# Reordering the halves, turns and rotations between and inside two layers, and starting the experts' gates two units later

## The reference

```
h    = rms_norm(x, g_mix[layer])
qkv  = h @ w_in[layer]                       # 1024 x 3072
o_a, o_b, o_c = differential, moba and dilated attention (rotary q and k), 4 + 4 + 8 heads
x    = x + concat(o_a, o_b, o_c) @ w_out[layer]
h2   = rms_norm(x, g_ffn[layer])
x    = x + (silu(gate) * val) @ w_down[layer],   gate, val = conv3(h2 @ w_up[layer])
```

## Time and profile before

| | us |
|---|---|
| median of three executions | 1775.79 |
| lowest, highest | 1773.83, 1776.22 |
| the profiled execution, its own time | 1779.4 |
| its span, first to last instruction | 1777.5 |
| mean granted clock of TensorE | 0.989 of full speed |
| PE busy | 1702.1 (96%) |
| DVE, ACT, POOL busy | 1146.9 (65%), 820.8 (46%), 705.2 (40%) |
| first layer, second layer, second block up to the experts, experts | about 0 to 352, 352 to 690, 690 to 986, 986 to 1777 |

### The profile page before, as it was taken

The page is one execution under the profiler, slowest core; times in us unless marked ns, Lnnn a source line. Parts: engine busy times, 40 slices in busy tenths (PEclk is TensorE's granted clock), DMA queues, the critical chain, the costliest instruction groups (busy, mean ns, idle before and its releaser), DMA issues.

```text
span 1777.5 us, 27226 instructions
## 1 busy us (share of the span) xinstructions
PE 1702.1 (96%) x10714; PEld 1461.6 (82%) x10714; DVE 1146.9 (65%) x2426; ACT 820.8 (46%) x1451; POOL 705.2 (40%) x384
## 2 busy tenths in 40 slices
PE   7999999989999999988999999899999999999997
PEld 5778998767799987543569999899999988888885
DVE  6654785746457666567332799999999644444444
ACT  5445655344466643011443554444444445445443
POOL 2324667043256740333144799700000144444442
PEclk9999999999999999999999999999999999999999
DMA  7333555553245554323345556544444566666664
GB/s 289 107 101 113 178 179 179 164 190 107 95 154 178 190 190 155 114 80 95 95 143 201 178 166 197 171 144 143 143 143 143 158 188 198 192 197 192 189 193 139
DMA packets 77455, 283.20 MB, mean 159 GB/s; under 512 B 8720, under 2 KB 8976, under 8 KB 77072
## 3 DMA queue, kind: packets, MB, share of 16 engines
q1 hardware_dynamic: 76032, 276.50, 48.2%
q10 hardware_dynamic: 1296, 4.97, 0.7%
HBM read 279.33 MB, written 2.10 MB: 158 GB/s over the span
## 4 chain that ended last, share of the span: by engine, by line
PE 70%; DVE 17%; ACT 5%; issue 4%; POOL 3%; DMA 1%; POOLq 0%; DVEq 0%; ACTq 0%
PE bank L538 55%; PE bank L529 7%; PE bank L593 5%; DVE H L1437 2%; ACT wh L1090 2%; POOL wl L2096 2%; DVE att L1448 2%; DVE H L1970 1%; DVE H L1976 1%; DVE H L1972 1%; ACT att L1093 1%; DVE wl L1431 1%; DVE H L1968 1%; DVE H L1974 1%; PE bank L661 1%
## 5 line engine op out<-in xcount | busy, mean ns | idle before, releaser
L2096 POOL TENSOR_TENSOR wl<-raw,wh 128x1024 fp32r<-128x1024 f32 x213 | 545.8, 2573 | 723.5 <-ACT wh L1090 701.8
L538 PE MATMUL bank<-hh,wh 128*128 128x256 f32 x1856 | 526.4, 284 | 3.8 <-POOL wl L2096 3.0
L1090 ACT ACTIVATE wh<-raw 128x1024 fp32r<-128x1024 f32 x476 | 492.6, 1050 | 62.0 <-PE bank L538 47.8
L538 PE MATMUL bank<-hl,wh 128*128 128x256 f32 x1856 | 519.7, 280 | 0.0
L538 PE MATMUL bank<-hh,wl 128*128 128x256 f32 x1856 | 518.7, 279 | 0.0
L1431 DVE TENSOR_TENSOR wl<-raw,wh 128x1024 fp32r<-128x1024 f32 x263 | 349.8, 1336 | 96.6 <-ACT wh L1090 96.2
L538 PEld LDWEIGHTS bank<-hh,wh 128*128 128x128 f32 x1856 | 349.8, 188 | 4.9 <-POOL wl L2096 3.9
L538 PEld LDWEIGHTS bank<-hl,wh 128*128 128x128 f32 x1856 | 349.8, 188 | 0.0
L538 PEld LDWEIGHTS bank<-hh,wl 128*128 128x128 f32 x1856 | 349.6, 188 | 0.0
L1437 DVE TENSOR_TENSOR acl<-H,ach 128x256 fp32r<-128x256 f32 x128 | 87.5, 684 | 181.6 <-ACT ach L1093 181.6
L538 PE MATMUL bank<-wh,ach 128*128 128x512 f32 x512 | 199.3, 389 | 0.4 <-DVE acl L1437 0.4
(11 more groups left out here) (217 smaller groups left out, 2326.1 us busy)
## 6 DMA issues: line engine op xcount, KB each, us to landing
raw<-in_ut_dram SPq DMA_DIRECT2D x128, 512.0 KB, 3.5
raw<-in_vt_dram SPq DMA_DIRECT2D x128, 512.0 KB, 3.6
raw<-in_wup_dram SPq DMA_DIRECT2D x88, 512.0 KB, 4.1
raw<-in_win_dram SPq DMA_DIRECT2D x48, 512.0 KB, 4.4
raw<-in_wdown_dram SPq DMA_DIRECT2D x44, 512.0 KB, 4.2
raw<-in_wout_dram SPq DMA_DIRECT2D x24, 512.0 KB, 3.6
raw<-in_wga_dram SPq DMA_DIRECT2D x16, 512.0 KB, 3.5
raw<-in_wpq_dram SPq DMA_DIRECT2D x16, 512.0 KB, 4.7
```

Of the source, the lines that this page charges most:

```text
L538: m = p.e.matmul(out, lhs[i][a], rhs[i][b], start=start and i == 0 and j == 0, stop=stop and i == n - 1 and j == 2)
L1090: a.e.activation(high_of(u), raw_of(u), ACTF.Copy).then_inc(act_hi.up(("hi", u)), 1)
L2096: g.e.tensor_tensor(low_of(u), raw_of(u), high_of(u).bitcast(F32), ALU.subtract).then_inc(pool_lo.up(("lo", u)), 1)
```

## The change

It touches only the order and the place of work; no operation is added or taken away.

1. `J_TURN` (29, 55) becomes (30, 57) and `J_GATE` 57 becomes 59. The low halves of ut units 57 and 58 go from DVE to POOL with it.
2. The causal group's turn of the attention output (`OUT_TURNS`) moves from behind w_out's unit 5 to ahead of it, on PE, ACT and DVE, in both layers.
3. In both layers ACT and DVE copy the turned q and k ahead of `stream` of the same step.
4. POOL rotates the causal group ahead of its `stream` of w_in's unit 23, in both layers.
5. Between the layers: the low halves of w_in's units 1 and 3 of layer 1 go from POOL to DVE; POOL no longer leaves out `stream` at w_down's units 19 and 20; DVE's `stream` of w_down's last unit comes behind the norm of tile 1; ACT and DVE drop `stream` of the row behind it, so that these halves come a step later; PE turns tile 1 ahead of unit 3 for tile 0 instead of behind it; DVE makes tile 1's low half ahead of its copy of the slab's first bank.

```
-        J_TURN = (29, 55)
-        J_GATE, N_GR = 57, 64
+        J_TURN = (30, 57)
+        J_GATE, N_GR = 59, 64
...
+            elif i in (first["win", 1] + 1, first["win", 1] + 3):
                 lower.append("d")
...
-        OUT_TURNS = {0: (DIFF, DIL0), 1: (DIL1, ), 6: (CAUSAL, )}
+        OUT_TURNS = {0: (DIFF, DIL0), 1: (DIL1, ), 5: (CAUSAL, )}
...                                                      # by_tokens
+                        if n in skew[:1] and (h, t) == at and between:
+                            between()
                         if t == 0:
                             unit(i)
-                        elif n in skew[:1] and h == 0 and between:
-                            between()
...                                                      # pe, w_in of layer 1
-                                  between=(lambda: turned(("n", 1), mix, 8, (1,), ...)) if L else None)
+                                  between=(lambda: turned(("n", 1), mix, 8, (1,), ...)) if L else None, at=(3, 0))
...                                                      # pe; act and dve alike
+                    if j == 5:
+                        for g in OUT_TURNS[5]:
+                            out_turned(g, (0, ))
                     out_unit(j, (0, 1), between)
-                for g in OUT_TURNS[6]:
-                    out_turned(g, (0, ))
...                                                      # act and dve, step k of w_in
+                    qk_turned(QK_TURNS.get(k, ()))
                     stream(first["win", L] + k)
...
-                    qk_turned(QK_TURNS.get(k, ()))
...                                                      # act, behind w_down
-                stream(first["row", "n", 1] if L == 0 else first["row", "g"])
+                if L:
+                    stream(first["row", "g"])
...                                                      # dve, k == 0 of layer 1
+                        turned(("n", 1), (1,), 2)
                         v.wait_ge(pe_out, ("mm", ("win", L), 0, 0))
                         copy(qkv[:, 0, 0:512], ps(("win", L), 0, 0), ("ev", "win", L, 0, 0), alone=True)
-                        turned(("n", 1), (1,), 2)
...                                                      # dve, w_down
-                    if t:
+                    if t and (L or f < NTILE - 1):
                         stream(first["wdown", L] + f)
...
                             scale(("n", 1), t, mix, first["row", "n", 1])
-                stream(first["row", "n", 1] if L == 0 else first["row", "g"])
+                            if t:
+                                stream(first["wdown", L] + f)
+                if L:
+                    stream(first["row", "g"])
...                                                      # pool, step k of w_in
-                    stream(first["win", L] + k)
+                    if k < 23:
+                        stream(first["win", L] + k)
                     if k in ROPES and ROPES[k] != DIFF:
...
+                    if k == 23:
+                        stream(first["win", L] + k)
...                                                      # pool, w_down
-                    if t and f not in (NTILE - 3, NTILE - 2):
+                    if t:
                         stream(first["wdown", L] + f)
```

More of the change, by code:

```diff
@@ L235, in program @@
             elif first["ut"] <= i < first["vt"]:
+                lower.append("d")
+            elif i in (first["win", 1] + 1, first["win", 1] + 3):
                 lower.append("d")
@@ L570, in turned_whole, with by_tokens @@
                         emptied[b] = (dve_out if q else act_out, ("hT", st, t, q))
-            def by_tokens(tag, u0, n_slabs, cw, nu, kper, off, ready, empties, of=range(8), skew=(), between=None, whole=hTw):
+            def by_tokens(tag, u0, n_slabs, cw, nu, kper, off, ready, empties, of=range(8), skew=(), between=None, at=(0, 1), whole=hTw):
                 for n in range(n_slabs):
@@ L754, in pe @@
                                   lambda n, t: (act_out if t else dve_out, ("ev", "win", L, n, t)), of=slab_banks, skew=(0,),
-                                  between=(lambda: turned(("n", 1), mix, 8, (1,), lambda t, q: (dve_out, ("nrm", ("n", 1), t, q)))) if L else None)
+                                  between=(lambda: turned(("n", 1), mix, 8, (1,), lambda t, q: (dve_out, ("nrm", ("n", 1), t, q)))) if L else None, at=(3, 0))
                 for k in range(24):
@@ L1202, in act @@
                         att_step(c)
+                    if j == 5:
+                        for g in OUT_TURNS[5]:
+                            out_turned(g)
                     stream(first["wout", L] + j)
-                for g in OUT_TURNS[6]:
-                    out_turned(g)
                 st, ev = ("f", L), ("xa", L)
```

## The result

| | before | after |
|---|---|---|
| median of four executions each, us | 1774.81 | 1756.65 |
| lowest, highest | 1773.7, 1776.22 | 1754.88, 1757.62 |
| the profiled execution, its span | 1779.4, 1777.5 | 1756.8, 1755.0 |
| mean granted clock in it | 0.989 | 0.993 |

The ratio is 0.9896, with a 95% interval of 0.9879 to 0.9913: faster by about 18.4 us (15.4 to 21.5). Forecast were 1752.6 and 1748.0 to 1761.5: the measured 1756.65 lies inside, 4.1 us above the forecast. The forecast gain, 23.2 us, lies above the interval of the measured one. The two spans differ by 22.5 us, 0.7 less than that; the medians differ by only 18.2. Where the missing 4 to 5 us went is the question of the experiments.

A forecast was written before the change was run, and what follows sets the result against it. PE was taken to bound the kernel, busy 1702.1 of 1777.5 us, losing time to stalls and low clock. Terms 7.1 + 5.6 + 3.0 + 3.3 + 4.2 = 23.2 off 1775.8 gave 1752.6 us, range 1748.0 to 1761.5.

The forecast's parts named there:

- border: Between the layers, low halves shared by DVE and POOL start tile 1 sooner: 7.1 us (5.4 to 8.0).
- experts: At the second routing, slabs 55 and 56 fill PE's 5.73 us wait: 5.6 us gained (4.0 to 7.0).
- causal turn: In both layers, w_out's unit 5 covers the turn, copy and low half: 2 x 1.50 = 3.0 us (1.5 to 3.0).
- rotation: In layer 0, POOL's rotation ahead of the low half removes PE's 1.73 us wait and low clock: 3.3 us (1.7 to 3.5).
- copies: Copying turned q and k ahead of low halves shortens PE's waits, with low clock: 4.2 us (1.5 to 4.5).
- Rival (a): At the border, DVE's unit 1 waits for POOL's unit 0: gain there 5.4, total 21.5, 1754.3 us; chance 0.15.
- Rival (d): In the gates, DVE's longer turn sets the pace, from a mean of 4.06 us; slower than before; chance 0.02.
- PE had stood still 1.73 us or longer just before: Reading of the profile before: clock falls follow such stalls, and none follows the stalls of 1.50 us or less.
- clock term: Low clock counted behind stalls: copies 1.56, rotation 1.6, border 3.0, experts 1.5, together 7.7 us of the sum.
- Rival (b): The clock's falls move to the shorter stalls that stay: 15.5 us gained, 1760.3 us; chance 0.12, with cases between.

The follow-up runs named there:

- the whole change without part 4: The changed kernel with POOL making the low half ahead of the causal group's rotation again: 1757.96 us on average.
- the transposes in the routing: The kernel before plus 45 transposes of a constant on PE in the wait of 5.73 us for the second routing: ratio 0.9984.
- parts 1, 2, 3 and 5 alone: Four runs, each the kernel before with one edit: between the layers 0.9955, experts' turns and gates 0.9970, causal turn 0.9982, q and k copies ahead of halves 0.9977.
- part 3: The kernel before with only the causal turn moved ahead of w_out's unit 5, on PE, ACT and DVE: ratio 0.9982.
- the border part alone: The kernel before with only the changes between the layers: ratio 0.9955, from five executions.
- part 2: The kernel before with only the experts' change, turns at 30 and 57 and gates from 59: ratio 0.9970.
- parts 1, 2, 4 and 5 alone: Four runs, each the kernel before with one edit: between the layers 0.9955, experts 0.9970, POOL's rotation ahead of the low half 0.9995, copies ahead of halves 0.9977.

## Why the prediction held, and where it failed

| step | forecast | measured alone | in the two profiles |
|---|---|---|---|
| border | 7.1 | 8.0 (5.2 to 10.8) | 7.3 |
| experts | 5.6 | 5.3 (3.4 to 7.5) | 5.2 |
| causal turn | 3.0 | 3.2 (1.4 to 4.8) | 2 x 1.50 |
| rotation | 3.3 | 0.9 (-1.1 to 2.8) | 3.1 (profile of the part alone) |
| copies | 4.2 | 4.1 (2.0 to 6.2) | |
| sum, or the whole | 23.2 | 21.5; whole 21.6 | 22.5 |

The last column: border as worked out above; experts from a matmul in the first routing to the first one of the second table, 1417.03 - 1066.46 = 350.57 before (the earlier trace rows has the latter) and 1394.10 - 1048.73 = 345.37 after. The lines, first of before, then two of after:

```profile
1417.03 0.47 PE L538 MATMUL bank<-wh,ach 128*128 128x512 f32 x1 [0.39 <-DVE acl L1437]
...
1048.73 0.39 PE L540 MATMUL bank<-hh,wh 128*128 128x256 f32 x1 [1.33 <-POOL wl L2105]
1394.10 0.47 PE L540 MATMUL bank<-wh,ach 128*128 128x512 f32 x1 [0.39 <-DVE acl L1442]
```

Four terms came out within 1 us, with intervals of 2 to 3 us to either side, and the parts add up to the whole. That the spans of the two profiles differ by nearly the forecast sum is in part luck: 1.5 of the 22.5 us comes between the same matmuls of the second block up to the experts (after is 698.02 - 681.76 = 16.3 us ahead at its first wait, and 1066.46 - 1048.73 = 17.7 ahead in the experts), which no edit touches.

- **Border, right.** DVE first, POOL blocked, no idle time over 1 us, clock 1.00. Rival (a) didn't come about: the low half of DVE took 1.22 us and not 2.14.
- **Experts, right in kind.** Two waits on POOL, forecast as 0.9 and 0.9, measured 0.31 and 1.29: 1.6 against the forecast 1.7 in sum (0.9 + 0.9, rounded). The first unit came sooner and the second later, as the profile's first routing had it (0.29 and 1.29). DVE's longer turns in the gates cost nothing that shows: from the first group of gates to the second table after takes 1394.10 - 1144.28 = 249.82 us, and before 1417.03 - 1161.61 (the end of the earlier trace rows's last line) = 255.42 with two more slabs of 2.81, so 249.80 without them. Rival (d) is far off.
- **Rotation, the term that was mis-sized.** The prediction gave 1.7 for the stall and 1.6 for the clock behind it, as if every execution paid the fall. The stage gained 3.1 in the profile, and the kernel 0.9 on average, 1.3 inside the whole change. The stall's part stands (1.64 in the profiles of the whole change with and without it). The clock's part was counted at its full 1.6, and most executions seem not to pay it: the same wait of 1.73 to 1.75 us is in seven profiles (before, the whole change without part 4, the transposes in the routing, and parts 1, 2, 3 and 5 alone), and the fall stands behind it in two of them (before, part 3).
- **"PE had stood still 1.73 us or longer just before", the reading under every clock term.** It held in the one profile of before, as long as PE had work (one more fall, at 1769 to 1776, comes behind its last matmul and costs nothing). It isn't a rule: in the profile of the border part alone PE stands still 1.74 us at 66.70, as in before at 66.68, and the clock stays. The window there, first of before:

```profile
66.00:74.00 8.00, 6.97 (x32) 5.43 (x32) 2.85 (x10) 2.83 (x7) 3.35 (x2) 0.79 0.28 73
```

  The same window with the border part alone:

```profile
66.00:74.00 8.00, 6.61 (x42) 5.12 (x42) 3.33 (x13) 3.12 (x7) 3.35 (x2) 1.00 0.27 71
```

  And the kernel after shows falls without a long stall, the first behind 1.09 us (at 397.11, a wait that before has too, 1.08 at 412.61, there with 1.00), the second while PE was busy all the time. Two windows of the kernel after:

```profile
396.00:406.00 10.00, 8.23 (x43) 6.32 (x42) 3.55 (x11) 3.21 (x8) 3.37 (x2) 0.83 0.23 75
736.00:746.00 10.00, 10.00 (x43) 5.34 (x43) 6.37 (x7) 0.20 (x1) 5.23 (x6) 0.66 0.24 81
```

  The program is the same in two profiles of the whole change, and even so the falls differ. The same two windows of the second one (the run of the whole change again), and the second of them in the first one, where the fall is missing:

```profile
396.00:406.00 10.00, 8.64 (x54) 6.93 (x55) 5.13 (x16) 3.82 (x10) 3.11 (x2) 1.00 0.22 61
786.00:796.00 10.00, 7.35 (x40) 3.31 (x39) 9.51 (x20) 1.68 (x3) 4.69 (x2) 0.83 0.17 52
...
786.00:796.00 10.00, 7.36 (x43) 3.56 (x44) 9.38 (x21) 1.68 (x3) 4.70 (x2) 1.00 0.17 52
```

  What the profiles show of the four clock terms is how often each is paid where its stall was left as it was: behind 1.74 us at 66.68 in 4 of 7 profiles, behind the rotation's 1.73 in 2 of 7, behind the border's 4.64 in 7 of 7 (in two of them for a shorter time), behind the routing's 5.73 in 6 of 6. So the two long stalls always had their fall and the two short ones only sometimes. With these shares the forecast's clock terms would be 1.56 x 4/7 + 1.6 x 2/7 + 3.0 + 1.5 = 5.9 instead of 7.7, and the sum 21.4, where 21.6 was measured; this is an estimate made after the fact, from few profiles.

  Rival (b), that the falls go elsewhere, would have cost 7.7 us, and the whole is 1.6 short (23.2 forecast, 21.6 measured). Falls at places where before has none do occur (412 and 698 in the profile of part 2), but that the stalls which stayed brought them about isn't shown. Split by the slope of 1.71 us for each 0.001, the five parts alone give 5.5 us of clock and 16.0 of the rest, where the forecast had 7.7 and 15.5. The whole change (mean clock 0.9893 to 0.9938) gives 7.7 and 13.9. The two splits differ by 2 us, which is within their error, so by the times alone which side the 1.6 is missing on stays open.
- **From the sum to the time, the step that made most of the 4 us.** The prediction took the sum off the median of three (1775.8), since "the stalls are in the program's order and not in that difference". True of the stalls; but 7.7 us of the sum were low clock, and what sets one execution of before apart from another is low clock too (1.71 us for each 0.001). The median of three lies 2.5 us below the mean of 67, by the slope a sample with little of it (the clocks of those three are not on record; the four executions of after that were measured with them average 1756.45, and the four of later 1756.86, so it wasn't a chip on which everything is faster). So the forecast's 4.1 us are 2.5 of a low starting point and 1.6 of a sum too large. Taken off the profiled execution the same sum gives 1756.2, where after's eight executions have 1756.66 on average; the prediction had this number and put it aside. That it comes so close is in part luck: the profiled execution lies 1.1 above the mean of 67, which makes up for most of the 1.6.

What is shown is that the low clock makes most of the spread, and that a stall of one length may or may not be followed by it. Not shown is what decides. Leaving out the fall behind PE's last matmul, the profiles of before and of part 3 alone have the same six falls; those of parts 1, 2, 4 and 5 alone lack one or more of them at stalls that the part left as they were. The Trainium skill (TensorE: Matmul & The Clock Gate, Part 1: The HAM clock gate) says that the number of matmuls at the low clock at a kernel's start varies from run to run. The number at the start wasn't looked at here; what varies here lies in mid-kernel, as the two profiles of one program show, and the mean granted clock was 0.986 to 0.992 over the 67 executions of before.

## What to carry to other kernels

Sum the idle time of a stall at its full length, but the low clock behind it only at the share of executions that pay it, and take that sum off a mean of many executions. Where there is one profile only and the clock terms are in it at full size, take the sum off the execution whose rows it was read from. Don't mix the two. Where three engines feed PE at a border between stages, give the first units to two of them (5.7 us here). Look also where the norm's short steps stand among the long halves: with three halves on POOL ahead of it the root of tile 1 came at 349.12 and DVE's `scale` waited 2.96 us for it, though moving the root by itself wasn't tried. A few transposes of a constant in a wait that can't be removed can be worth more than the wait suggests, but look in the timeline that they lie in it.

## What the runs showed of the hardware that was not expected

- One stall, several outcomes: 1.74 us idle at 66 to 67 was followed by a clock of 0.79 over 66 to 74 in before, and by 1.00 in the profile of the border part alone; over all seven profiles with this stall the fall came four times. Two profiles of the same program (the whole change) don't agree on it at 397 and at 790 either.
- A fall with PE at 10.00 of 10.00 us busy (736 to 746, clock 0.66), amid matmuls on 32 rows. It cost next to nothing: PE's wait for the table behind it was 1.42 us instead of 4.33 before, so the slow work ran in time that would have been idle. From the 32-row matmuls to the turn behind the wait it is 748.62 - 737.35 = 11.27 us after and 764.55 - 753.60 = 10.95 before. The turn, first of before, then of after:

```profile
764.55 0.44 PE L885 MATMUL bank<-ids,tab 128*128 128x128 f32 x2 [4.33 <-ACT tab L1093]
...
748.62 0.44 PE L888 MATMUL bank<-ids,tab 128*128 128x128 f32 x2 [1.42 <-ACT tab L1096]
```

- A fall behind a wait of 3.50 us in the state-space stage was kept away by work that computes nothing, at a gain of 3.5 us in the mean of 4 against 8 executions. All twelve profiles without this work have the fall, while behind the shorter waits (1.74 us at 66.68, 1.73 at 125.75) it comes and goes.
